# Weighting expert rows as they are copied out, adding gathers, and scattering the tokens of the last two blocks

## What is computed

```python
xn2 = rmsnorm(x, ffn_norm_w)                       # (1088, 1024)
g_logits = xn2 @ w_rg + b_rg;  grp = argmax(g_logits);  p_grp = softmax(g_logits)[grp]
e_logits = (xn2 @ w_re + b_re)[group grp]          # 8 experts in each of 4 groups
top_v, top_i = top_k(e_logits, 2)
w = softmax(top_v) * p_grp                         # two weights a token
h = silu(xn2 @ w_gate[e]) * (xn2 @ w_up[e])        # for each of the token's 2 experts
y = x + w[0] * (h0 @ w_down[e0]) + w[1] * (h1 @ w_down[e1])
```

## Time and profile before

| | us |
|---|---|
| median of 3 runs | 1494.5 |
| lowest, highest | 1493.59, 1495.94 |
| span of the profiled execution | 1493.6 |
| its last PE matmul ends at about | 1455.6 |
| PE busy | 1415.8 |
| DVE busy | 1001.7 |
| ACT busy | 726.6 |
| POOL busy | 210.4 |

### The profile page before, as it was taken

The page is one execution under the profiler, slowest core; times in us unless marked ns, Lnnn a source line. Parts: engine busy times, 40 slices in busy tenths (PEclk is TensorE's granted clock), DMA queues, the critical chain, the costliest instruction groups (busy, mean ns, idle before and its releaser), DMA issues.

```text
span 1493.6 us, 21566 instructions
## 1 busy us (share of the span) xinstructions
PE 1415.8 (95%) x8064; PEld 1198.3 (80%) x8064; DVE 1001.7 (67%) x1342; ACT 726.6 (49%) x862; POOL 210.4 (14%) x243
## 2 busy tenths in 40 slices
PE   7999999999999998999999889999999999999990
PEld 7899999989999998899888666777777777777760
DVE  4422321167666667776566688888888888888875
ACT  6421121144444445423211157777777777777760
POOL 2600000021111111000200040231111111111024
PEclk9999999999999999999999799999999999999995
DMA  6346323244333324658721389999999999999948
GB/s 200 120 152 212 119 80 70 75 136 129 122 115 112 109 68 119 196 172 251 284 83 42 133 325 380 374 378 400 392 389 395 389 388 397 396 396 395 363 137 310
DMA packets 135911, 347.40 MB, mean 233 GB/s; under 512 B 13784, under 2 KB 92060, under 8 KB 110176
## 3 DMA queue, kind: packets, MB, share of 16 engines
q1 hardware_dynamic: 125688, 312.32, 58.0%
q0 software_dynamic: 6048, 21.50, 4.7%
q10 hardware_dynamic: 4120, 12.85, 2.2%
HBM read 292.34 MB, written 55.28 MB: 233 GB/s over the span
## 4 chain that ended last, share of the span: by engine, by line
PE 45%; DVE 3%; DMA 2%; ACT 1%; POOL 1%; issue 1%; POOLq 0%; ACTq 0%; DVEq 0%
PE xt_ey L2595 4%; PE xt_ey L2596 4%; PE xt_ey L2597 4%; PE y_h_up L2574 4%; PE y_h_up L2573 4%; PE y_h_up L2575 4%; PE logits_gate L2573 2%; PE logits_gate L2575 2%; PE logits_gate L2574 2%; PE ranks_gate L2573 2%; PE ranks_gate L2575 2%; PE ranks_gate L2574 2%; PE y_x L2562 2%; DVE e_w_lo L2454 1%; PE y_x L2119 1%; PE y_h_up L2119 1%
## 5 line engine op out<-in xcount | busy, mean ns | idle before, releaser
L2454 DVE TENSOR_TENSOR e_w_lo<-mixed,e_w_hi 128x2048 fp32r<-128x2048 f32 x64 | 145.8, 2296 | 0.5 <-ACT e_w_hi L2387 0.5
L2454 DVE TENSOR_TENSOR e_w_lo<-w_out,e_w_hi 128x2048 fp32r<-128x2048 f32 x64 | 143.6, 2285 | 2.9 <-ACT e_w_hi L2387 2.9
L1008 PE MATMUL gate_banks<-f_hi,wg_hi 128*128 128x364 f32 (+1 forms) x376 | 126.8, 337 | 0.9 <-DVE wg_lo L876 0.4
L2387 ACT CAST e_w_hi<-mixed 128x2048 fp32r<-128x2048 f32 x62 | 117.0, 1913 | 14.0 <-ACT e_y_rows L2408 8.9
L1009 PE MATMUL gate_banks<-f_lo,wg_hi 128*128 128x364 f32 (+1 forms) x376 | 123.5, 328 | 0.0
L1010 PE MATMUL gate_banks<-f_hi,wg_lo 128*128 128x364 f32 (+1 forms) x376 | 123.4, 328 | 0.0
L2387 ACT CAST e_w_hi<-w_out 128x2048 fp32r<-128x2048 f32 x64 | 121.9, 1906 | 0.6 <-ACT e_y_rows L2408 0.6
L2595 PE MATMUL xt_ey<-e_w_hi,e_hT_hi 128*96 128x512 f32 x256 | 102.8, 402 | 4.2 <-DVE e_w_lo L2454 3.9
L2314 POOL CAST idx<-token_of_slot 96x1 uint32 (+1 forms) x30 | 48.6, 1620 | 402.0 <-PE y_x L2562 368.7
L2596 PE MATMUL xt_ey<-e_w_lo,e_hT_hi 128*96 128x512 f32 x256 | 101.5, 396 | 0.0
L2573 PE MATMUL y_h_up<-e_w_hi,e_x_hi 128*96 128x512 f32 x256 | 100.8, 394 | 0.8 <-DVE e_w_lo L2454 0.8
(11 more groups left out here) (634 smaller groups left out, 3604.7 us busy)
## 6 DMA issues: line engine op xcount, KB each, us to landing
w_out<-in_w_down_e SPq DMA_DIRECT2D x64, 1024.0 KB, 9.1
mixed<-in_w_gate_e SPq DMA_DIRECT2D x32, 1024.0 KB, 8.7
mixed<-in_w_up_e SPq DMA_DIRECT2D x32, 1024.0 KB, 9.4
w_gate<-in_w_gate_e SPq DMA_DIRECT2D x32, 1024.0 KB, 8.1
w_up<-in_w_up_e SPq DMA_DIRECT2D x32, 1024.0 KB, 8.7
expert_rows<-e_y_rows ACTq DMA_DIRECT2D x32, 384.0 KB, 7.3
proj<-mixed SPq DMA_DIRECT2D x8, 1408.0 KB, 5.6
w_ring<-in_w_in SPq DMA_DIRECT2D x7, 1408.0 KB, 10.7
```

Source lines behind the costliest of these rows:

```text
L1008: pe.matmul(bank, wg_hi[j][:, k, :], hi, start=(k == 0), stop=False)
L2387: act.copy(hi(i, step, j), raw(i, u, j)).then_inc(hi_ready[i], 1)
L2454: dve.tensor_tensor(lo(i, u, j), raw(i, u, j), hi(i, step, j).bitcast(F32), ALU.subtract).then_inc(lo_ready[i], 1)
```

## The change

It has four parts.

- **Weights.** PE also builds a table `weight_of` of each slot's weight (18 small matmuls in `home_rows` with the one-hot rows scaled on DVE), and ACT's `down_out` multiplies by it as it copies out. `expert_rows` then holds weighted rows.
- **Adding gathers.** The 18 gathers at the end name `x2` itself as their destination and add to it (`compute_op=ALU.add`). The 18 weighted additions on DVE are gone. The first nine start when block 28 (2·more-2) is stored, the second nine when block 29 is.
- **The last two blocks by slot.** Tokens with a row in block 30 or 31 are finished slot by slot: POOL gathers their residual (from a new copy `x2d` in HBM) and their other row into `whole[0]` and `whole[1]`, DVE adds the block's own result, and four indirect DMAs scatter them into `y_prompt` and `y_sample` after the plain stores of `y` have landed. Blocks 29 and 30 are stored behind the other rows (`late`); their normal places and that of block 31 hold zeros.
- **Slot table by scatter.** Instead of `choice`, `labels` and `labels_taken`, POOL scatters four facts for each of a token's two slots (token, weight, row of its other result) into `slot_info` in HBM (`info_rows`, 18 indirect DMAs spread over the gathers of blocks 2 to 4) and loads the table back. DVE takes tokens and weights of the extra blocks from it in `labels_out`, now in block 5, and `experts_out` is now in block 2. POOL's `late_rows`, 11 small operations, stands between the wait for `labels_ready` and the loop of gathers.

The core of the diff:

```diff
+            sp.dma_start(a["x2d"][1 + t * P:1 + t * P + r, :], R.x2[:r, t, :]).then_inc(R.x2_stored, 16)
...
-        dve.wait_ge(R.numbers_ready, 1)
...
+        for j in range(2):
+            ins = dve.tensor_tensor(hot_tok[:, j], hot[:, j], bc(R.weight[:, :, j], 2, NE), ALU.mult)
+        ins.then_inc(s["weighted_ready"], 1)
...
-        spare_products(24)
+        spare_products(8)
+        pe.wait_ge(s["weighted_ready"], 1)
+        home_rows(range(NR), True, True, WOF).then_inc(s["weights_full"], 1)
+        spare_products(4)
...
         for b in range(2, 6):
             pool.wait_ge(s["xT_full"], b - 1)
             gather(b, b % 2)
+            if b < 5:
+                if b == 2:
+                    pool.wait_ge(R.ordered, 1)
+                    pool.wait_ge(R.labelled, 1)
+                info_rows(parts[b - 2])
+            if b == 4:
+                pool.wait_ge(s["info_stored"], 16 * 2 * NR)
+                pool.wait_ge(s["experts_known"], 1)
+                pool.dma_start(table[:], ...).then_inc(s["table_loaded"], 16)
         pool.wait_ge(s["labels_ready"], 1)
         more = pairs_after_first(pool)
+        late_rows(more)
         with pool.Fori(2, more) as tt:
...
+        for t in range(NR):
+            add_rows(0, t)
+        pool.wait_ge(done[GATE], 4 * more + 2)
+        seen()
+        for i in range(2):
+            pool.indirect_dma_start(whole[i][:], None, a["x2d"], ...).then_inc(late_x_loaded[i], 16)
         pool.wait_ge(stored[1], 16 * more)
+        for t in range(NR):
+            pool.wait_ge(rows_added[0][t], 16)
+            add_rows(1, t)
...
+        pool.wait_ge(y_stored, 16 * NR)
+        pool.wait_ge(late_ready[0], 1)
+        late_out(0)
+        pool.wait_ge(late_stored, 32)
+        pool.wait_ge(late_ready[1], 1)
+        late_out(1)
+        pool.wait_ge(late_stored, 64)
...
-            act.copy(yb[u][:], Y[:SLOTS, :]).then_inc(s["y_act"], 1)
+            act.activation(yb[u][:], Y[:SLOTS, :], ACT.Copy, scale=R.weight_of[:, bass.ds(b, 1)]).then_inc(s["y_act"], 1)
...
         step(1, 1)
-        step(2, 0, lambda: choice(0))
-        step(3, 1, lambda: choice(1))
-        step(4, 0, labels_out, labels_taken)
-        step(5, 1, experts_out)
+        step(2, 0, experts_out)
+        step(3, 1)
+        step(4, 0)
+        step(5, 1, labels_out)
...
-        step(2, 0, 1, 1, choice=0)
-        step(3, 1, 1, 2, choice=1)
+        step(2, 0, 1, 1)
+        step(3, 1, 1, 2)
```

More of the change, by code:

```diff
@@ L57 @@
 AHEAD = 3
+INFO = 4
+SKIPPED = 8192.0
 PIECE = KD * FE // 2
-WORK = 36736
+WORK = 36192
 TCH = [(0, 512), (512, 512), (1024, TS)]
@@ L1772, in choices_in_order @@
         L = own.link
-        low_row, high_row, swap = rank[:, 0:NR], rank[:, NR:], extra[:, 0:NR]
-        w, moved = [R.weight[:, :, j] for j in range(2)], [home_row[:, j * NR:(j + 1) * NR] for j in range(2)]
-        dve.wait_ge(R.numbers_ready, 1)
+        low_row, high_row, both_rows = rank[:, 0:NR], rank[:, NR:], rank[:]
+        more, third_last, second_last, last, shift = gs[:], m1[:], m2[:], dm[:], gh[:]
+        moved, kept = extra[:], home_row[:]
         dve.tensor_tensor(low_row, dest[:, 0:NR], dest[:, NR:], ALU.min)
@@ new lines, in choices_in_order @@
+        dve.tensor_scalar(third_last, more, 2.0 * SLOTS, -float(SLOTS), ALU.mult, ALU.add)
+        dve.tensor_scalar(second_last, more, 2.0 * SLOTS, None, ALU.mult)
+        dve.tensor_scalar(last, more, 2.0 * SLOTS, float(SLOTS), ALU.mult, ALU.add)
+        L(dve.tensor_scalar(shift, more, -2.0 * SLOTS, float((MAXB + 1) * SLOTS), ALU.mult, ALU.add))
+        dve.tensor_scalar(moved[:, 0:NR], high_row, third_last, shift, ALU.is_ge, ALU.mult)
+        L(dve.tensor_scalar(moved[:, NR:], high_row, second_last, shift, ALU.is_ge, ALU.mult))
@@ L2346, in on_gpsimd @@
                 gather(2 * tt + 2 + u, u)
-        def gather_rows(n):
-            blocks = a["expert_rows"][0:(MAXB + n) * SLOTS, :]
-            for t in range(NR):
-                r = tile_rows(t)
-                pool.indirect_dma_start(rows[n][t][:r], None, blocks,
-                                        bass.IndirectOffsetOnAxis(ap=R.row_of[:r, n * NR + t:n * NR + t + 1], axis=0)).then_inc(rows_loaded[n][t], 16)
-        pool.wait_ge(R.ordered, 1)
-        pool.wait_ge(s["xT_full"], 2 * more + 2)
@@ L2434, in on_scalar @@
         act.wait_ge(R.ordered, 1)
-        step(1, 1, 0, 0)
+        act.wait_ge(R.weights_known, 1)
+        step(1, 1, 0, 0, first=True)
+        for b in range(2, 6):
+            step(b, b % 2, b // 2, (b - 1) // 2)
+        act.wait_ge(s["labels_ready"], 1)
         more = pairs_after_first(act)
-        with act.Fori(1, more) as tt:
+        with act.Fori(3, more) as tt:
             step(2 * tt, 0, tt, tt - 1)
@@ L2441, in on_scalar @@
         step(end - 1, 0, more, more - 1)
-        step(end, 1, more, more, True)
-        down_out(end - 1, 0, more)
+        step(end, 1, more, more, end=True, late=0)
+        down_out(end - 1, 0, more, 1)
         for j in range(2):
@@ L2446, in on_scalar @@
         h_split(end)
-        down_out(end, 1, more, True)
     def on_vector(dve):
@@ L2469, in hidden, with step @@
             dve.tensor_tensor(h[:], silu[:], Up[:SLOTS, :], ALU.mult).then_inc(s["h_ready"], 1)
-        def step(b, u, piece=None, taken=None, end=False):
+        def step(b, u, piece=None, end=False):
             p = b - 1
             split(GATE, b, u, 0, u)
-            if taken is not None:
-                taken()
             hidden(p)
@@ L2598, in down, with step @@
                 ins.then_inc(done[DOWN], 1)
-        def labels(j):
-            pe.wait_ge(s["choice_ready"], j + 1)
-            for t in range(NR):
-                ins = pe.matmul(LAB[:SLOTS, 2 * NX * j:2 * NX * (j + 1)], s_hot[:, t, :], b_tok[:, t, :], start=(t == 0), stop=(t == NR - 1))
-            ins.then_inc(s["choice_full"], 1)
-        def step(b, u, tt, next_tt, first=False, choice=None):
+        def step(b, u, tt, next_tt, first=False):
             hidden(GATE, b, u, 0, Gt[u])
@@ L2614, in step @@
             down(b - 1, 1 - u, u, first)
-            hidden(UP, b, u, 0, Up)
-            if choice is not None:
-                labels(choice)
-            hidden(UP, b, u, 1, Up)
+            for j in range(2):
+                hidden(UP, b, u, j, Up)
         turn(0, 0, 0, True)
```

217 lines of the change are left out of this document (121 added, 96 removed).

## The result

| | before | changed |
|---|---|---|
| median of 4 runs each, same chip | 1495.22 us | 1523.06 us |
| lowest to highest | 1493.59 to 1495.97 | 1519.40 to 1524.54 |
| span of the profiled execution | 1493.6 us | 1522.8 us |

The ratio is 1.0187, with a 95% interval of 1.0169 to 1.0205. The changed kernel is 27.8 us slower; forecast were 21 (1515.5 against 1494.5), in a range of 1491 to 1526 us.

A forecast was written before the change was run, and what follows sets the result against it. PE, never idle mid expert stage, and the 38 us of gathers, additions and stores behind its last matmul bound the kernel. 1493.6 + 0.5 - 2.7 + 13.3 + 3.1 + 6.8 = 1514.6, as median 1515.5 us; range 1491 to 1526.

The forecast's parts named there:

- Start of the stage and blocks 2 to 5: Block 0: extra DVE work on PE's path, +0.5 us; blocks 2 to 5: removed choices, labels and DVE inserts, -2.7 us.
- which the trace's slack just takes: Blocks 2 to 4: six scatters at 1.6 us each delay following gathers up to 10 us, without stopping PE.
- The stall at block 6: Block 6's transposes: late labels and eleven late_rows operations delay the gather, PE waits +13.3 us, between 7.4 and 17.
- PE's clock: Behind block 6's stall: granted clock drops, 6 us of matmuls at half speed, +3.1 us, at most 8.5.
- The end: Behind the last blocks: DMA bounds y, then late_out scatters and program end follow; +6.8 us, from -12.6 to +13.2.
- The head start: End: first adding gather starts after block 28's store, 31 us earlier than before, some 26 us before block 30's copy.
- second read: End: adding gathers also fetch old x2 bytes; upper bound 25.8 us, three quarters taken, 19.4 us.
- program's end: After the last scatters land: the end of the program takes 1.3 us, as in the kernel before.
- (a): End: adding gathers cost the plain price, all else as forecast; 1496 us, chance 0.22.
- (b): End: head start wins with plain-price additions and a short block 6 stall of 7.4 us; about 1488 us, chance 0.15.
- (c): End and block 6: full price of the second read and 8.5 us of low clock; 1527 us, chance 0.13.
- (d): Block 6: rows come in time, no stall, only the dear gathers count; 1499 us, chance 0.05.

The follow-up runs named there:

- the four kernels built on it: Against the kernel before: scattered table and weighted copies alone, 1492.5 us; also first nine gathers adding, 1487.6; also nine skipping adding gathers, 1497.0; those interleaved, 1494.4.
- the kernel without stalls: Changed kernel with late_rows behind the loop of gathers, table load behind block 5's gather and labels_out in step 4: 1503.8 us.
- plain gathers: Changed kernel with the 18 gathers into x2 fetching without adding, so the residual is left out of y: 1507.8 us.
- the two pairs of kernels: Kernel before without and with POOL waiting for y's stores: 1494.2, 1499.4 us; changed kernel without late_out, with and without POOL's waits: 1511.0, 1504.6.
- a third pass: Kernel before with scattered table, weighted copies, first nine gathers adding, plus nine adding gathers for late first choices, skipping other rows: 1497.0 us; interleaved 1494.4.
- one move: Changed kernel with only late_rows moved from ahead of the loop of gathers to behind it: 1517.6 us.
- the other: Changed kernel with table load behind block 5's gather and labels_out in step 4, late_rows left ahead of the loop: 1516.6 us.

## Why the prediction was right in sign and short in size

- **Start of the stage and blocks 2 to 5** (+0.5 and -2.7): the -2.7 is right. Without the stalls stretch A is 2.4 us shorter than before in one profile (542.1), and 0.9 to 4.5 shorter in the four kernels built on it. The +0.5 falls ahead of block 0's copy, where the spread hides it. The step that failed is "which the trace's slack just takes". I sized a scatter at 1.6 us from the gathers' spacing at the end; beside DVE's low parts the 18 took 2.23 us each in the mean with 0.30 between, and as each six held up the next, the gather of block 5 came not 10 but 29.7 us late. The wait for their landing, which stands on POOL ahead of that gather, I had not counted. And by the forecast's own rows the slack did not suffice: 16.6 us less 10 are under the median landing of 8.6 us. Price: 3.09 us of PE, and a drop of the clock.
- **The stall at block 6** (+13.3): 11.10 us, by the steps named: labels late, two of eleven operations blocked (2.32 and 2.13 us), nine short ones, gather issued at 976.58, landed 4.2 us later. I had added 6.3 for the landing; the queue was dry. With block 5's the two stalls make 14.2 us against the forecast 13.3; that these come so near is luck, for one of them was not forecast. The lower bound of 7.4 is 7.7 when its terms are added up. And the forecast treated the late labels and the eleven operations as a plain sum, which they are not: together they are worth more than each alone.
- **PE's clock** (+3.1): A has 13.5 + 2.4 = 15.9 us over the kernel without stalls; 12.6 of them are waits of PE in A (15.9 against 3.3), which leaves 3.3. The size is right, its place only in part: the forecast had 6 us of work at 1.2 GHz behind block 6, where the profile has 4.3 (PE works from 980.93, and 985 to 990 is at 0.98), and 3.4 more lie behind the unforeseen stall of block 5. Half of 7.7 is 3.9. The windows behind block 6's stall:

```profile
975.00:980.00 5.00, 0.00 (x0) 0.00 (x0) 0.00 (x0) 0.00 (x0) 2.46 (x5) 0.50 0.33 96
980.00:985.00 5.00, 4.07 (x15) 3.17 (x16) 0.96 (x1) 2.49 (x2) 1.10 (x2) 0.50 0.29 83
985.00:990.00 5.00, 5.00 (x23) 3.46 (x22) 4.86 (x3) 4.64 (x5) 0.00 (x0) 0.98 0.73 210
```

  So the block stage was forecast at +13.7 (without the +0.5 that falls ahead of it) and measured at +13.5, within a spread of some 4 us.
- **The end** (+6.8, measured +13.7). The head start came as forecast: the first adding gather was issued 26.1 us ahead of block 30's copy. By the terms: y out 46.1 us behind that copy, measured 48.2. In this two errors met: plain gathers would have needed 31.0, not 26.7, and the additions, the forecast's second read, cost 17.2, not 19.4. The scatters took 9.6, not 11.6. The **program's end** was taken at 1.3 us "as it does now" (the profile before has 1.7) and took 8.0: this is the term that was mis-sized, by 6.7 us, and it is nearly all of what the forecast lacks. Some 4 of the 6.7 are POOL's end by the two pairs of kernels; some 2 come with the changed kernels in another way that was not found. The 1.3 us was read from a kernel in which POOL had issued its last gather 18 us before the end. The change made POOL the last engine, and that has a price of its own.
- **Rivals.** (a), plain price, is refuted by the plain gathers: 1507.8 us in their place. (b) wanted a short stall and a gain at the end; without any stall the kernel still took 1503.8 us, since the end gives nothing while y waits for adding gathers and POOL ends last. (c) came out nearest in time, 1527, but for another reason: the second read did not cost its full price, and the clock cost 3 to 4 us and not 8.5. (d) is refuted by the stall itself.

The Trainium skill, "Collectives: The Full Stack", section "The bandwidth ceiling: the fold count and why AG ≠ RS ≠ AR", has a ReduceScatter, whose additions read two sources, at 1/1.93 of an AllGather, which copies; here the gathers that add into SBUF ran at 204 GB/s, 1/1.5 of the plain ones beside the same stores and 1/1.64 of those in the earlier trace rows. The direction agrees, the measured factor decides. The forecast worked out 1523 us by that figure, and 1523.1 were measured, by luck: its term is 27 us where 17.2 were found, and the program's end made up for most of the difference. The Trainium skill, "SBUF — State Buffer", section "Who interferes with whom", has the second of two instructions wait for the first; the rows of 2.13 to 6.93 us for operations of 0.2 us agree, and they show it across several DVE instructions in a row.

## What to carry to other kernels

Before work is moved into a DMA that adds, count the old bytes as a transfer too: it costs 17 us where the gathers are what the end waits for. Where the queues have room (the first nine gathers beside blocks 29 to 31) it brought 5 us, but in a kernel that leaves some rows out; made complete by a third pass, it was no faster than the kernel before. Ask of a step behind a stall whether it is the cause or only sheltered by it: here one move brought 5 to 6 us, the other 6, both 19. Take the clock of a profile along when two kernels are compared: a shorter stall can look like nothing when the clock stays low for longer. And look at who is last: a single wait that made POOL finish with the last store cost 5 us with no work in it.

## What the runs showed of the hardware that was not expected

- A POOL that finishes last makes the end of the program later by some 4 us in the profiles (SP's last wait 4.3 in place of 0.2 us, and 6.4 in place of 2.0), 5.2 and 6.4 us in the medians, the second with other differences in it.
- What POOL pays for an indirect DMA does not go by its bytes: 0.96 us for 128 rows of 16 bytes, 0.94 us for 128 rows of 4 KB. An adding one took 1.53 us, and still 1.55 us with nearly all its rows skipped by the bound, while it moved next to nothing.
- A POOL operation of 0.2 us on 96 x 2 elements took 6.93 us over three DVE instructions in a row.
- A gather of block rows lands 4.2 us behind its issue when the queues have run dry and takes 8 to 9 us under the weight loads (8.9 in the median of the changed kernel). Issued 5.4 us sooner behind the labels, while the loads ran, it landed only 1.4 us sooner.
- Short stalls of PE at the same place, in kernels with the same code up to there, were followed by different clocks: 3.09 us by a mean granted clock of 0.83 in 950 to 960, 2.61 us by 0.80 and 0.86 in 940 to 960, 2.28 us by 1.00 throughout.
